# Per-head keys and values, column-half value products and a deeper probability pipeline in the second block's attention

## The reference

```python
c = rms_norm(c_kv, kv_g)                              # (S, 128): one latent row for each position
q_lat = einsum('bshd,hcd->bshc', qh, w_uk) * 64**-0.5 # 8 heads, d = 64, c = 128
# an indexer picks 256 keys for each query; the others are masked
s = einsum('bthc,btkc->bthk', q_lat, c_sel)
s = where(valid, s, neg)
p = softmax(s, axis=-1)
o_lat = einsum('bthk,btkc->bthc', p, c_sel)
att = einsum('bshc,hcd->bshd', o_lat, w_uv)           # (S, 8*64)
...
mixed = concatenate([att * silu(gate_a), ssm * silu(gate_s)], -1)
y = einsum('bse,ed->bsd', mixed, w_out)               # 1024 x 1024
out = layer_norm(ALPHA * x + y, ln_g, ln_b)
```

## Time and profile before

| | |
|---|---|
| time, median of 3 runs | 2802.92 us (2799.8 to 2815.97) |
| the profiled execution's own time | 2806.37 us |
| its span in the profile | 2804.3 us |
| PE busy | 2602.3 us (93%) |
| DVE busy | 1328.1 us (47%) |
| ACT busy | 826.2 us (29%) |
| POOL busy | 347.4 us (12%) |
| granted clock of PE, mean | 0.977 |

### The profile page before, as it was taken

How to read it: one execution, slowest core, us unless ns; L and a number is a source line. 1 busy time by engine, 2 the same in 40 slices (tenths; PEclk the granted TensorE clock), 3 DMA queues, 4 the chain that set the end, 5 groups by cost and what they waited for, 6 DMA issues and landing times.

```text
span 2804.3 us, 31977 instructions
## 1 busy us (share of the span) xinstructions
PE 2602.3 (93%) x12253; PEld 1804.6 (64%) x12253; DVE 1328.1 (47%) x2130; ACT 826.2 (29%) x1485; POOL 347.4 (12%) x463
## 2 busy tenths in 40 slices
PE   6998998799999979989988999999989999989998
PEld 4855777686666868557776866668547555445553
DVE  3253565321112242536653211122679989955763
ACT  3232445311112232324453111121251212133341
POOL 0012221000000000122210000000043753100000
PEclk9998999999999989989999999999999999999999
DMA  5010000211112030100002111120400011010000
GB/s 188 27 61 1 1 1 1 61 46 45 45 45 86 34 125 27 61 1 1 1 1 61 46 45 45 45 99 22 129 31 9 31 39 38 30 61 31 30 16 30
DMA packets 106281, 119.04 MB, mean 42 GB/s; under 512 B 20592, under 2 KB 76624, under 8 KB 106128
## 3 DMA queue, kind: packets, MB, share of 16 engines
q1 hardware_dynamic: 106128, 116.96, 13.3%
HBM read 98.92 MB, written 16.84 MB: 41 GB/s over the span
## 4 chain that ended last, share of the span: by engine, by line
PE 77%; DVE 8%; issue 6%; ACT 6%; DMA 1%; POOL 1%; SPq 1%; ACTq 0%; DVEq 0%; POOLq 0%
PE PS L649 8%; PE PS L619 6%; PE PS L622 6%; PE PS L625 6%; PE PS L741 5%; PE PS L446 4%; DVE negm L1697 4%; PE PS L970 4%; PE PS L580 2%; PE PS L663 2%; PE PS L666 2%; PE PS L669 2%; PE PS L883 2%; PE PS L556 2%; PE PS L838 2%
## 5 line engine op out<-in xcount | busy, mean ns | idle before, releaser
L619 PE MATMUL PS<-hHi,R2bR 128*128 128x512 f32 x768 | 306.6, 399 | 15.7 <-ACT rows L1303 15.7
L622 PE MATMUL PS<-hLo,R2bR 128*128 128x512 f32 x768 | 300.5, 391 | 0.0
L625 PE MATMUL PS<-hHi,R2bR 128*128 128x512 f32 x768 | 300.2, 391 | 0.0
L1271 ACT ACTIVATE R2b<-PS,negm 128x1024 f32<-128x1024 f32 x128 | 142.6, 1114 | 210.1 <-DVE negm L1697 210.1
L1716 DVE TENSOR_TENSOR R2bR<-W,R2bR 128x1024 fp32r<-128x1024 f32 x48 | 57.5, 1222 | 309.1 <-ACT R2bR L1291 309.1
L580 PE MATMUL PS<-R2b,R 128*64 128x128 f32 x2048 | 129.0, 279 | 56.8 <-ACT R2b L1276 56.8
L1323 ACT ACTIVATE R3a<-PS,pT 128x512 f32<-128x512 f32 x64 | 42.3, 687 | 467.4 <-PE PS L625 467.4
L1697 DVE TENSOR_REDUCE negm<-PS 128x1 f32<-128x1024 f32 x128 | 155.8, 1217 | 46.8 <-PE PS L556 46.8
L619 PEld LDWEIGHTS PS<-hHi,R2bR 128*128 128x128 f32 x768 | 145.3, 189 | 49.2 <-ACT hHi L1262 16.1
L580 PEld LDWEIGHTS PS<-R2b,R 128*64 128x64 f32 x2048 | 115.3, 139 | 82.0 <-issue 80.1
L622 PEld LDWEIGHTS PS<-hLo,R2bR 128*128 128x128 f32 x768 | 145.4, 189 | 33.1 <-issue 3.3
(11 more groups left out here) (347 smaller groups left out, 4812.8 us busy)
## 6 DMA issues: line engine op xcount, KB each, us to landing
W<-in_w_in SPq DMA_DIRECT2D x10, 2048.0 KB, 8.2
W<-in_w_in SPq DMA_DIRECT2D x33, 512.0 KB, 4.7
xres<-R SPq DMA_DIRECT2D x3, 4096.0 KB, 19.3
W<-in_w_out SPq DMA_DIRECT2D x6, 2048.0 KB, 7.8
R<-xres SPq DMA_DIRECT2D x2, 4096.0 KB, 18.9
W<-in_c_dft_s SPq DMA_DIRECT2D x2, 2052.0 KB, 8.8
R<-in_x SPq DMA_DIRECT2D x1, 4096.0 KB, 13.1
W<-in_w_in SPq DMA_DIRECT2D x4, 1024.0 KB, 7.4
```

The costliest lines, as they stand in the source:

```text
L619: mm = pe.matmul(o, wHi[c % 2][:, k, :], hHi[:, k, ns], start=(k == 0), stop=False)
L622: mm = pe.matmul(o, wHi[c % 2][:, k, :], hLo[:, k, ns], start=False, stop=False)
L625: mm = pe.matmul(o, wLo[c % 2][:, k, :], hHi[:, k, ns], start=False, stop=(k == 7))
L1271: act.activation(Pb[u % 2], PS[:, b:b + 2, :].rearrange("p a c -> p (a c)"), ACT.Exp, bias=negm[:, u:u + 1], accum_out=rsum[:, u:u + 1]).t ...
```

## The change

`c W_uk` and `c W_uv` are computed once (`kT2`, eight products of 512 columns; `v2`, another eight), in place of the queries' product with `w_uk`, and in place of `latent_out`, `att_out` and `att_turn` in the loop. The loop on PE now goes over 32 pairs `p` of heads. `scores2(p)` does both heads of a pair from 64 rows of depth each, one in the upper and one in the lower rows of the array, into banks 0, 1 and 2, 3; the next pair needs both. `pv_pair2(p)` multiplies values and probabilities, two heads side by side in the array's column halves, and leaves the attention turned, so that no transpose follows. The softmax sums therefore have to be divided along the other axis: DVE inverts them (`sums_inverted`), SP writes them to DRAM and reads them back spread over the partitions (`rbc`), and `att_gate` multiplies by them. There are four buffers `Pb2` and four `PT2` instead of two, and the copies `turned` run two units behind. All `out_half` go to bank 7 in the loop; those with `n = 0` come one tile later (`t - 2`). `ln_std` moves from `h == 2` to `h == 6`, `layer_norm` from `h == 4` to `h == 7`, and of `LATE` the entry `h == 3` becomes `h == 2`.

```diff
-LATE = [(3, 7)] + [(t, h) for t in (4, 5, 6) for h in (1, 3, 5, 6, 7)]
+LATE = [(3, 7)] + [(t, h) for t in (4, 5, 6) for h in (1, 2, 5, 6, 7)]
...
+        kT2 = r0[:, 0:4096].rearrange("p (m s) -> p m s", m=4)
+        v2 = r0[:, 4096:8192].rearrange("p (t c) -> p t c", t=NT)
+        Pb2 = [r3b[:, 0:1024], r3b[:, 1024:2048], r2b[:, 1024:2048], r2b[:, 2048:3072]]
+        PT2 = [hTf[:, i * 1024:(i + 1) * 1024] for i in range(4)]
+        rbc = [hTf[:, 7168 + 512 * i:7680 + 512 * i].rearrange("p (m c) -> p m c", m=4) for i in range(2)]
...
(PE)
             for m in range(4):
                 for n in range(2):
                     b = 2 * m + n
                     o = begin(b)
+                    pe.matmul(o, wuk[:, m * P:(m + 1) * P], c2T[:, n * 512:(n + 1) * 512],
+                              start=True, stop=True).then_inc(full[b], 1)
+            pe.nop().then_inc(w_used[1], 1)
+            pe.wait_ge(s2_wv, 16)
+            for t in range(NT):
+                o = begin(t)
+                pe.matmul(o, c2T[:, t * P:(t + 1) * P], wuv, start=True, stop=True).then_inc(full[t], 1)
...
+            def scores2(p):
+                t, m = p // 4, p % 4
+                begin(0)
+                begin(2)
                 w = (t + 1) * P
                 for n in range((w + 511) // 512):
+                    for e in range(2):
+                        r_ = slice(VD * e, VD * e + VD)
+                        mm = pe.matmul(PS[:, 2 * e + n, 0:min(512, w - 512 * n)], qT2[r_, m, t * P:(t + 1) * P],
+                                       kT2[r_, m, n * 512:min(w, n * 512 + 512)], start=True, stop=True)
+                        if n == (w - 1) // 512:
+                            mm.then_inc(full[2 * e], 1)
...
+            def pv_pair2(p):
+                t, m = p // 4, p % 4
+                pe.wait_ge(free[4], pt2[2 * p + 1][0])
+                pe.wait_ge(free[5], pt2[2 * p + 1][1])
+                if m == 0:
+                    begin(6)
                 for k in range(t + 1):
+                    for e in range(2):
+                        h = 2 * m + e
+                        mm = pe.matmul(PS[VD * e:VD * e + VD, 6, m * P:(m + 1) * P], v2[:, k, h * VD:(h + 1) * VD],
+                                       PT2[(2 * p + e) % 4][:, k * P:(k + 1) * P], start=(k == 0), stop=(k == t))
+                if m == 3:
+                    mm.then_inc(full[6], 1)
...
             scores2(0)
+            for p in range(4 * NT):
+                t, m = p // 4, p % 4
+                if p + 1 < 4 * NT:
+                    scores2(p + 1)
+                p_turn2(2 * p)
+                if p >= 1:
+                    pv_pair2(p - 1)
+                if m < 2 and t >= 2:
+                    out_half(t - 2, 0, m)
+                if m >= 2 and t >= 1:
+                    out_half(t - 1, 1, m - 2)
+                p_turn2(2 * p + 1)
+            pv_pair2(4 * NT - 1)
+            for half in range(2):
+                out_half(NT - 2, 0, half)
+            for half in range(2):
+                out_half(NT - 1, 1, half, 4)
+            for half in range(2):
+                out_half(NT - 1, 0, half, 5)
...
(SP)
-            sp.wait_ge(full[0], marks["qlat"])
+            for b in range(8):
+                sp.wait_ge(full[b], marks["attention"][b])
             small(lng, a["ln_g_2"][0].partition_broadcast(P), s2_ln)
             small(lnb, a["ln_b_2"][0].partition_broadcast(P), s2_ln)
...
+                sp.wait_ge(s2_ri, t + 1)
+                for e in range(2):
+                    sp.dma_start(rsums2[t, e].rearrange("m q -> q m"), rinv[:, H * t + e:H * t + H:2],
+                                 allow_slow_non_contiguous=True).then_inc(s2_rw, 16)
+                sp.wait_ge(s2_rw, 32 * (t + 1))
+                for e in range(2):
+                    small(rbc[t % 2][VD * e:VD * e + VD].rearrange("p m c -> p (m c)"),
+                          rsums2[t, e].rearrange("m q -> (m q)").partition_broadcast(VD), s2_bc)
...
(ACT: kT2 out of all eight banks, v2 out of the even ones; in the loop)
+                act.activation(Pb2[u % 4][:, 0:w], Pb2[u % 4][:, 0:w], ACT.Exp, scale=-1.0,
                                bias=negm[:, u:u + 1], accum_out=rsum[:, u:u + 1]).then_inc(free[b], 1)
+                if u >= 2:
+                    turned_high(u - 2)
+                if t >= 2 and h == 6:
                     ln_std(t - 2)
...
(DVE: v2 out of the odd banks; in the loop)
+            def sums_inverted(t):
                 dve.wait_ge(free[2], sums2[t])
+                dve.reciprocal(rinv[:, H * t:H * t + H], rsum[:, H * t:H * t + H]).then_inc(s2_ri, 1)

             def att_gate(t):
                 o = arrive(6)
+                dve.wait_ge(s2_bc, 32 * (t + 1))
+                dve.tensor_tensor(att, o.rearrange("p (m c) -> p m c", m=4), rbc[t % 2], ALU.mult).then_inc(free[6], 1)
+                dve.wait_ge(free[6], bk.count(6))
                 m = mix[:, 0:4, t * P:(t + 1) * P]
+                dve.tensor_tensor(m, m, att, ALU.mult).then_inc(s2_gate, 1)
...
+                if u >= 2:
+                    turned(u - 2)
...
                 if t >= 2:
                     if h == 0:
+                        residual(t - 2, 1)
+                    if h == 4:
                         residual(t - 2, 0)
+                    if h == 7:
                         layer_norm(t - 2)
                 if t >= 1:
                     if h == 1:
+                        sums_inverted(t - 1)
                     if h == 3:
                         att_gate(t - 1)
+            for u in (H * NT - 2, H * NT - 1):
+                turned(u)
+            sums_inverted(NT - 1)
+            residual(NT - 2, 1)
             residual(NT - 2, 0)
             att_gate(NT - 1)
             layer_norm(NT - 2)
+            residual(NT - 1, 1, 4)
+            residual(NT - 1, 0, 5)
             layer_norm(NT - 1)
```

More of the change, by code:

```diff
@@ L294, in build @@
         xres = nc.dram_tensor("xres", (S, D), F32, kind="Internal").ap()
+        rsums2 = nc.dram_tensor("rsums2", (NT, 2, H // 2, P), F32, kind="Internal").ap()
         rsums = nc.dram_tensor("rsums", (H, S), F32, kind="Internal").ap()
@@ L888, in _ @@
             gates(5, 0)
-            qT_free = [bk.count(b) for b in range(8)]
             pe.wait_ge(s2_wk, 16)
-            o = begin(0)
             for m in range(4):
[L893 to L899, removed]
                 for n in range(2):
-                    b = (1 + 2 * h + n) % 8
+                    b = 2 * m + n
                     o = begin(b)
-                    r_ = slice(VD * (h % 2), VD * (h % 2) + VD)
-                    pe.matmul(o, wukT[r_, h // 2, :], qT2[r_, h // 2, n * 512:(n + 1) * 512],
+                    pe.matmul(o, wuk[:, m * P:(m + 1) * P], c2T[:, n * 512:(n + 1) * 512],
                               start=True, stop=True).then_inc(full[b], 1)
-            marks["qlat"] = bk.count(0)
+            pe.nop().then_inc(w_used[1], 1)
[3 more added lines that the diff above has]
+                pe.matmul(o, c2T[:, t * P:(t + 1) * P], wuv, start=True, stop=True).then_inc(full[t], 1)
             marks["attention"] = list(bk.n)
@@ L930, in p_turn2 @@
                     for c in range(4 * j, min(4 * j + 4, t + 1)):
-                        mm = pe.transpose(o[:, (c % 4) * P:(c % 4 + 1) * P], Pb2[u % 2][:, c * P:(c + 1) * P], ident[:, :])
+                        mm = pe.transpose(o[:, (c % 4) * P:(c % 4 + 1) * P], Pb2[u % 4][:, c * P:(c + 1) * P], ident[:, :])
                     mm.then_inc(full[4 + j], 1)
                 pt2[u] = (bk.count(4), bk.count(5))
[L935 to L939, removed]
-                for k in range(t + 1):
-                    mm = pe.matmul(o, c2[:, k, :], PT2[hg][:, k, :], start=(k == 0), stop=(k == t))
-                mm.then_inc(full[6], 1)
-                ol_free[hg] = bk.count(6)
@@ L945, in att_out @@
[L945 to L959, removed]
@@ L963, in out_half @@
+            def out_half(t, n, half, b=7):
                 if (n, half) == (1, 0):
-                    pe.wait_ge(free[6], turn_free[0])
+                    pe.wait_ge(s2_gate, t + 1)
                     if t == 0:
@@ L967, in out_half @@
                 wo = k_of(weights2(6 + n)) if t == half == 0 else k_of(W[:, n, :])
-                o = begin(6 + n) if half == 0 else PS[:, 6 + n, :]
+                o = begin(b) if half == 0 else PS[:, b, :]
                 for k in range(4 * half, 4 * half + 4):
@@ L971, in out_half @@
                 if half == 1:
-                    mm.then_inc(full[6 + n], 1)
-            pt2, ol_free, turn_free = {}, {}, {}
+                    mm.then_inc(full[b], 1)
+            pt2, score_free = {}, {}
             scores2(0)
[L976 to L997, removed]
+            for p in range(4 * NT):
[17 more added lines that the diff above has]
+                out_half(NT - 1, 0, half, 5)
         @block.sync
@@ L1139, in _ @@
```

(18 more changed lines are left out.)

116 lines of the change are left out of this document (33 added, 83 removed).

## The result

The changed kernel takes 2856.2 us (median of 4 runs, 2854.5 to 2857.3) against 2804.5: the ratio is 1.0176, 95% interval 1.0143 to 1.0208. That is 1.8% slower, where 1.3% faster was forecast and the range ended at 2794.

A forecast was written before the change was run, and what follows sets the result against it. PE alone was taken to set the pace of late tiles. Loop -45.5, in front of it +5.4 and DRAM trip +4.6 gave -35.5 us, from 2802.9 to 2767 us; range for all 2748 to 2794.

The forecast's parts named there:

- PE's relief: Loop on PE: 144 us leave, 94 come back; of the 50 it is rid of, 45.5 show in the loop.
- the scores of two heads beside each other: PE, scores from 64 rows: two heads' products overlap, so a pair costs 1.81 us in tile 7.
- the values in the column halves: PE, values as in the first block: a pair costs 0.246 (t + 1) us.
- the price of a switch: PE, changing the array's division: 0.2 us a switch, four or 0.8 us a pair, 26 us in all.
- The sum of the pairs: Loop, pair by pair over eight tiles: 226 us, plus 7.8 for the last pair, 234 against 279.4.
- The sums' way through DRAM: SP's write and read of the sums: a 6.7 us trip, gate waiting in tiles 1 and 2 only, +4.6 us.
- Rival 1: DRAM round trip near its upper end of 12 us, every gate waits: +28 against the forecast, 2795; chance 0.10.
- The sign that I had named: Gate waits for the DMA of `rsums2` in tiles 1 and 2 alone; waits in late tiles would show the forecast wrong.
- the longest of three sums: Each pair in the loop takes the longest of PE, DVE from mask to mask, and the round.
- the round K: A pair's scores with switch, two maskings, copy and exponential in a row: 2.0 to 6.4 us in tiles 0 to 7.
- In front of the loop: Before the first masking: sixteen products come, L904 and the turning of `w_uk` go, +5.4 us.
- rival 3: PE waits in each pair and its clock falls to 1.2 GHz: slower, near 2850 with half slow; chance 0.05.

The follow-up runs named there:

- the version with the copy last: Changed kernel with division on POOL, residual one unit later, and DVE's odd-unit extra steps before the copy of the turned probabilities: 2772.1 us, ratio 0.9872.
- without the trip: Changed kernel with no writing or reading of sums through DRAM, the gate multiplying by a constant (division left out): 2805.4 us, ratio 1.0011.
- with the other waits gone: Changed kernel keeping its 4-byte DRAM write, with residual one unit later, reciprocal right behind the masking, odd-unit extra steps before the copy: 2810.8 us, ratio 1.0037.
- both edits: Changed kernel without the sums' way through DRAM (division left out) and with the residual one unit later on DVE: 2786.0 us, ratio 0.9938.

## Why the prediction was wrong, step by step

**Right.** What bounded the kernel before; PE's relief: the scores of two heads beside each other, the values in the column halves, the price of a switch. In the version with the copy last PE goes through two pairs of tile 7 like this:

```profile
2689.16 1.92 PE PS L921 x8
2691.08 1.02 PE PS L935 x8
2692.10 1.68 PE PS L949 x28
2693.78 3.63 PE PS L966 x8
2697.41 0.87 PE PS L935 x8
2698.28 1.92 PE PS L921 x8
2700.20 1.02 PE PS L935 x8
2701.22 1.90 PE PS L949 x32
2703.12 3.64 PE PS L966 x8
```

The first goes from scores to scores in 9.1 us. By the steps between instructions inside a group (0.43 us for two side by side of 512 columns, 0.109 for two of 128 and for a transpose, 0.43 for an instruction of the output) it would be 8.4, so four switches come to 0.7 and not 0.8. The next pair, with all 32 instructions of the values, takes 9.35 us (to 2707.6) for the 9.8 of the forecast, whose paces for scores and values were means over groups and held a switch already.

The sum of the pairs came near: 234 us forecast, 237.8 measured where the waits below are taken away (242 in two other profiles of that order). That is in part luck. Between the maskings of odd units the four pairs of tile 5 take 8.2, 10.5, 5.3 and 12.1 us, where the forecast had 9.3, 8.7, 8.4 and 9.3; the single errors cancel. (The residual stands one unit later in this order, which moves 0.7 and 2.9 us of DVE's work between pairs.)

**What the three edits are worth.** The loops of four profiles: 327.1 us in the changed kernel, 275.9 without the trip, 257.1 with the residual later too, 237.8 with the copy last. So of the 93 us between the forecast's loop and the measured one the trip is 51, the residual's place 19, the copy's place 19, and 4 are left. By the medians the steps are 51, 19 and 14.

**The sums' way through DRAM**, the term that was mis-sized: a trip of 12.4 to 14.4 us and not 6.7, against a bound of 12. A write of 512 pieces of 4 bytes, two of them side by side, lands in 8.4 us (median of all 16; 8.5 in the loop) and at most in 10.4, not in 2.5. I took the value next to the row with few large pieces, because the transfer is small in bytes. The Trainium skill's rule (DMA: Bandwidth & Descriptors, Rules for kernel authors), one descriptor for each element, spoke for the other end. The trace agrees: the two writes of tile 5 stand there as 1056 packets under 512 bytes, for 1024 elements, and 32 pieces in their place took 47 us off. The price on the kernel was 51 us (39 with the other waits gone), where the sum had 4.6. Rival 1 was this mechanism with 28 us more than the forecast, 33 in all. Its trip was too short, for DVE idled 43 us at the gate, and the other 8 us came on top of the gate's own waiting, which was all that I had counted. The sign that I had named, a gate that waits in late tiles, came: in tile 6 it waits 4.7 us.

**The order on DVE**, the step that failed in its mechanism. I took a pair's time as the longest of three sums, PE, DVE and the round, as if each engine could go on with its own work. It can't where an instruction that waits for PE stands in front of work that doesn't. There were two such places, and the code shows both. `residual(t - 2, 0)` at h = 4 waits for the output product that PE does in the same pair; I added its 2.9 us to the round K, but not the transposes, the values and the product before it. The copy of the odd unit waits for the transposes behind the output product, and the selection step and the layer norm stand behind it. By the run without the trip and the one with both edits, the first is worth 19 us; by the one with both edits and the one with the copy last, the second is worth 14 (19 by the loops). I named what is queued behind the gate, and didn't ask the same of the two other waits.

**In front of the loop** +5.4 was forecast, +1.0 came. The work itself costs what I said: from the start of the keys' product (2465.9) to the first masking 19.5 us pass, from the turning of `w_uk` (2470.0) it was 14.4 before, so +5.1. But in this execution PE comes to that work 4 us earlier than in the one before. In the other profiles with the keys' product that start lies anywhere from 2463.5 to 2481.0, with the same code in front; why it moves is open.

**The clock** (rival 3). PE ran at 1.2 GHz for 115 us of the changed kernel's loop; before, for 8. Without the trip it is 67 us, with the residual later too 50, with the copy last 25. Each slow stretch in the changed kernel's loop begins in a wait of PE or just behind one, and each of the six long waits for the gate has one. An output half of eight instructions takes 4.2 us there and 3.6 elsewhere. So rival 3 happened in part, as a consequence of the waits. How much of the 51 us is the slow clock isn't separated, since no run keeps the one without the other. An estimate from above: work done in 48 us (115 less 67) at half the clock takes 24 at full, so at most 24 of the 51.

## What to carry to other kernels

Price each wait on an engine by what stands behind it in that engine's stream, and put work that needs nothing in front of an instruction that waits. A maximum over busy sums is a lower bound, not a forecast, until each cross wait in a pair has been laid in order. A transfer's length goes by its pieces: a few KB in 4-byte pieces can take longer than half a MB in rows, so turn small tables on an engine before they are written.

## What was not expected of the hardware

- Two writes of 512 pieces of 4 bytes each, 4 KB in all, land 6.4 to 10.4 us after their issue (median 8.4); a load of 512 KB in rows takes 3.3 in the same kernel. Their packets lie within 1 us, as far as the profile shows, and the rest of the time is behind them.
- Products of two heads from 64 rows each run beside each other when they alternate one by one, too: 8 instructions of 512 columns in 1.92 us.
- POOL's multiplication of 128 x 768 by one number for each partition takes 2.2 us, more than its products of two tensors of that size in the first block (1.49 and 1.8), and was hidden all the same (a loop of 256.9 us with it, 257.1 without).

```profile
2626.10 2.20 POOL L2317 TENSOR_SCALAR R3b<-R3b,sums 128x768 f32<-128x768 f32 x1
```
